# Copies of U and the scaled key moved from VectorE to ScalarE in the mixing of a hybrid encoder

## The chip, the cores and the metric

The kernel runs on one core of a Trainium2 chip. The metric is the device time of one execution in microseconds (us), lower is better. A core has five engines that run side by side, each in the order of its own queue, and that wait for each other through semaphores: TensorE (PE in the profile, PEld its weight loads) multiplies matrices into PSUM; VectorE (DVE) and ScalarE (ACT) work elementwise and carry results out of PSUM; GpSimd (POOL) and SyncE (SP) issue transfers here.

## The reference

Two residual layers on 256 tokens of width 2048. The first mixes with an RWKV-7 recurrence over 32 heads of 64, the second with sparse attention; each is followed by a SwiGLU. The change is in the recurrence alone. Cut to that:

```python
def _rwkv7_scan(r, w, k, v, kk, a):
    def step(S, inp):
        r_t, w_t, k_t, v_t, kk_t, a_t = inp
        sa = jnp.einsum('bhij,bhj->bhi', S, -kk_t)
        S = (S * w_t[:, :, None, :]
             + sa[..., None] * (kk_t * a_t)[:, :, None, :]
             + v_t[..., None] * k_t[:, :, None, :])
        y = jnp.einsum('bhij,bhj->bhi', S, r_t)
        return S, y
...
    kk = heads(k * k_k)
    kk = kk / jnp.maximum(jnp.linalg.norm(kk, axis=-1, keepdims=True), 1e-12)
    k = k.astype(f32) * (1 + (a - 1) * k_a)
    y = _rwkv7_scan(r_h, w_h, k_h, v_h, kk, a_h)
```

The line `k * (1 + (a - 1) * k_a)` is the key that is scaled. Everything is float32.

## The kernel before

The program is a chain of phases. Before and after the mixing stand large linear layers, whose weights SyncE streams in, ScalarE and VectorE split into a high and a low part, and TensorE multiplies. The mixing (`rwkv`) computes the recurrence in chunks of 64 tokens: within a chunk through triangular matrices, between chunks through a state S.

It runs in eight rounds, i = 0 to 7. A round holds two column tiles, j = 0 and 1, of 128 columns (two heads each), and its 256 tokens as NC = 4 chunks. All rounds are written out, so that each engine has one straight list of instructions. A round has three stages on each engine, `stage_M`, `stage_N`, `stage_C`:

- `stage_M`: TensorE multiplies the decayed keys with each other, VectorE masks the result (XE, Dd, W).
- `stage_N`: the triangular inverse grows in W by repeated products. TensorE makes the powers DX2, DX4, D8B, TZ16, TZ32 and the turned values VK in PSUM; ScalarE copies them out (`evac`); VectorE adds to W (`grow`). In the same stage the next round's inputs are prepared (`prep_...` with i + 1): ScalarE makes q (`prep_v`) and the copies vb (`prep_values`) and the exponentials (`prep_exp`); VectorE runs `prep_a` (a running sum Ls) and `prep_b`, which makes the scaled key in the tile k2 (named `k` in the profile): first `a * k_a + (1 - k_a)`, line 2181, with the two columns `pv` and `omka`, then that times k, line 2164, then rb, line 2185.
- `stage_C`: the chain over the four chunks c. TensorE makes R, ScalarE copies it into Rr; TensorE multiplies it into U, VectorE copies it into Uu (line 2308); TensorE makes S and part of the output from Uu, ScalarE copies S scaled (line 2126); then the next chunk. In chunk 0 ScalarE also takes the next round's key norm (`prep_norm`: two logarithms, two exponentials, tile rk). In between VectorE prepares the next round (`prep_d`, `prep_e`) and does the modulation sums (`ada_half`, line 1954, tile `ada_ring`), eight in a round, whose rows SyncE loads. At the end of the stage ScalarE rounds an earlier round's y (`rounded`, tile hid) and then takes y out of PSUM (`take_y`, tile yc).

Nothing but these lists sets the order: an engine whose next instruction waits for a semaphore holds back all behind it. The helpers `at` and `past` write such waits; each instruction adds to a semaphore of its own name ("U", "S", "t1" for the scaled key).

Of the kernel before, what the change touches and what calls it, by code (L numbers as in the profile page):

```python
# [18 lines left out]
HD = 64  # L19
# [1548 lines left out]
class Program:  # L1568
# [22 lines left out]
    def s(self, name):  # L1591

        if name not in self.sems:
            self.sems[name] = self.nc.alloc_semaphore(name)
        return self.sems[name]
# [300 lines left out]
    def rwkv(self, loras):  # L1896
# [116 lines left out]
        def scalar(act):  # L2013
            def copy(name, dst, src, scale=1.0):
                nc.scalar.activation(dst, src, ACT.Copy, scale=scale).then_inc(s(name), 1)  # L2015
# [14 lines left out]
            def prep_values(i):  # L2030
                for j in range(2):
                    past(act, i, "VK")
                    copy("vb", R[j]["vb"][:], R[j]["in"][:, 2, :])

            def prep_exp(i):
                for j in range(2):
# [79 lines left out]
            def stage_C(i, post, prep):  # L2116
                for c in range(NC):
                    for j in range(2):
                        act.wait_ge(s("Rp"), i * 8 + (2 * c + j + 1))
                        copy("R", R[j]["Rr"][:], bank(j, 2, slice(c * HD, (c + 1) * HD)))  # L2120
                    if prep and c == 0:
                        prep_norm(i + 1)
                    if c < NC - 1:
                        for j in range(2):
                            act.wait_ge(s("Sp"), i * 6 + (2 * c + j + 1))
                            nc.scalar.activation(R[j]["S"][:], bank(j, 1, slice(c * HD, (c + 1) * HD)), ACT.Copy,
                                                 scale=R[j]["Pi_end"][:, c:c + 1]).then_inc(s("S"), 1)
                    elif post:
                        rounded(i - 1)
# [32 lines left out]
        def vector(dve):  # L2162
# [3 lines left out]
            def col(i, first, j):  # L2166
                return self.pv[:, bass.ds(i * 2 + (first + j), 1)]
# [7 lines left out]

            def prep_b(i, j):
                b = R[j]
                r, k, v, sw, a = (b["in"][:, n, :] for n in range(5))
                at(dve, i, "Ls", j)
                tt("Lx", b["Px"][:], b["Ls"][:], sw, SUB)  # L2180
                nc.vector.tensor_scalar(b["k2"][:], a, col(i, PV_KA, j), self.omka[:, bass.ds(i * 2 + j, 1)], MUL, ADD).then_inc(s("t1"), 1)
                at(dve, i, "t1", j)
                tt("k2", b["k2"][:], b["k2"][:], k, MUL)
                at(dve, i, "k2", j)
                nc.vector.scalar_tensor_tensor(b["rb"][:], r, col(i, PV_RK, j), b["k2"][:], MUL, MUL).then_inc(s("rb"), 1)
# [117 lines left out]

            def stage_C(i, q, post, prep):
                for c in range(NC):
                    for j in range(2):
                        dve.wait_ge(s("Up"), i * 8 + (2 * c + j + 1))
                        nc.vector.tensor_copy(R[j]["Uu"][:], bank(j, 3, slice(c * HD, (c + 1) * HD))).then_inc(s("U"), 1)
                    if c == 0:
                        if prep:  # L2310
                            for j in range(2):
                                prep_d(i + 1, 1 - q, j)
                        ada_sums(i)
                    if c in (1, 2) and prep:
                        prep_e(i + 1, 1 - q, c - 1)
                    if prep and c % 2:
                        adas(i + 1, c // 2)
                    if c == 2 and post:
                        gated(i - 1)
# [341 lines left out]
```

## Time and profile before

| | |
|---|---|
| median of the runs | 2681.77 us (2675.21 to 2682.4) |
| the profiled execution, first to last instruction (span) | 2683.1 us |
| mean granted TensorE clock | 0.987 |
| TensorE busy | 2569.3 us, 96% |
| VectorE busy | 1912.7 us, 71% |
| ScalarE busy | 1234.6 us, 46% |

The mixing's rounds lie between 387 and 723 us of the span. How the rows below are read: a *window* gives one stretch (us from the span's start) with its length, the busy time of PE, PEld, DVE, ACT and POOL (number of instructions in brackets), the granted TensorE clock as a share of full speed, the share of the DMA engines and GB/s. A row of *waits* gives who stood idle at which line, for whom, how long in total, how often, and the longest. A row of a *tile* gives an instruction with its count, its shortest, median and longest duration in ns and when the first and the last began. A row of a *timeline* gives start and duration in us, engine, line, operation, what is written from what, how many instructions are merged, and in square brackets the idle time of the engine just before and who ended it; without brackets the engine did not idle. "issue" is idle time for which the profile shows no one to wait for. Durations overlap a little from one instruction to the next.

### The profile page before, as it was taken

The numbers are of one execution on the slowest core, as the hardware profiler recorded it, in microseconds if no ns is written. First come the engines' busy times: TensorE is split into PE (matmuls) and PEld (weight loads), VectorE is DVE, ScalarE is ACT, GpSimd is POOL, SyncE is SP. The second block draws the span as 40 slices with busy tenths as digits, with TensorE's granted clock in tenths as the row PEclk, the third lists the DMA queues.
The fourth block names the chain that finished last, engine by engine and source line by source line (L and its number), as shares of the span: only waits on it lengthen the run. The fifth ranks groups of instructions, "written<-read, shape, count | busy, mean of one in ns | idle before, by whom it ended". The sixth has DMA issues, their size and how long they took to land.

```text
span 2683.1 us, 53108 instructions
## 1 busy us (share of the span) xinstructions
PE 2569.3 (96%) x20028; PEld 2254.2 (84%) x20028; DVE 1912.7 (71%) x2641; ACT 1234.6 (46%) x1886; POOL 46.5 (2%) x83
## 2 busy tenths in 40 slices
PE   7999998888899999999999999999999999999998
PEld 6888887778788888888888888887888888888887
DVE  6868746878687777777777776587887655555556
ACT  2245554444445444444444454344454444444445
POOL 2000020000000000000000000000000000000000
PEclk9999999999999999999999999999999999999999
DMA  9999775444196888888888668656788655666654
GB/s 402 414 327 308 258 255 175 149 152 133 55 318 218 283 284 290 278 282 282 294 278 283 218 220 282 235 207 208 261 282 281 211 189 182 188 195 189 186 164 141
DMA packets 443443, 640.96 MB, mean 239 GB/s; under 512 B 22049, under 2 KB 403105, under 8 KB 422433
## 3 DMA queue, kind: packets, MB, share of 16 engines
q1 hardware_dynamic: 439552, 626.35, 69.3%
q0 software_dynamic: 3744, 12.59, 1.3%
q8 instruction: 101, 1.65, 0.3%
q14 instruction: 46, 0.37, 0.0%
HBM read 624.18 MB, written 14.68 MB: 238 GB/s over the span
## 4 chain that ended last, share of the span: by engine, by line
PE 66%; DVE 4%; ACT 1%; DMA 1%; issue 1%; DVEq 0%; SPq 0%; ACTq 0%
PE ps L1784 43%; PE ps L1788 21%; DVE ada_ring L1830 1%; DVE wlo L1768 1%; DMA ada_ring<-in_ada 1%; ACT whi L1763 1%; DVE nt L131 0%; PE ps L1424 0%; PE ps L1418 0%; DVE act L144 0%; DVE st L1325 0%; PE ps L1457 0%; DVE lgf L1322 0%; PE ps L1449 0%; PE ps L1439 0%
## 5 line engine op out<-in xcount | busy, mean ns | idle before, releaser
L1768 DVE TENSOR_TENSOR wlo<-raw,whi 128x1024 fp32r<-128x1024 f32 (+1 forms) x736 | 865.8, 1192 | 444.6 <-ACT whi L1763 443.1
L1784 PE MATMUL ps<-act,whi 128*128 128x512 f32 x3528 | 1108.4, 395 | 1.6 <-DVE act L144 1.6
L1763 ACT ACTIVATE whi<-raw 128x1024 fp32r<-128x1024 f32 (+1 forms) x736 | 745.5, 1030 | 643.7 <-PE ps L1788 637.7
L1788 PEld LDWEIGHTS ps<-act,wlo 128*128 128x128 f32 x3528 | 662.7, 188 | 156.6
L1788 PE MATMUL ps<-act,wlo 128*128 128x256 f32 x3528 | 693.2, 278 | 0.0
L1784 PE MATMUL ps<-hid,whi 128*128 128x512 f32 x2176 | 680.7, 394 | 8.3 <-DVE wlo L1768 7.3
L1784 PEld LDWEIGHTS ps<-act,whi 128*128 128x128 f32 x3528 | 537.3, 189 | 2.4 <-DVE wlo L1768 2.0
L1788 PEld LDWEIGHTS ps<-hid,wlo 128*128 128x128 f32 x2176 | 410.3, 189 | 89.7
L1788 PE MATMUL ps<-hid,wlo 128*128 128x256 f32 x2176 | 433.0, 279 | 0.0
L1784 PEld LDWEIGHTS ps<-hid,whi 128*128 128x128 f32 x2176 | 332.3, 189 | 10.9 <-DVE wlo L1768 4.9
L1830 DVE SCALAR_TENSOR_TENSOR ada_ring<-ada_ring,silu 128x2048 f32<-128x2048 f32 x128 | 292.4, 2285 | 12.3 <-DMA ada_ring<-in_ada 12.3
L1133 PE MATMUL ps<-first_mix,raw 128*128 (+1 forms) x512 | 114.5, 386 | 7.0 <-DVE first_mix L1007 7.0
L1133 PEld LDWEIGHTS ps<-first_mix,raw 128*128 128x128 f32 x512 | 98.4, 193 | 23.1 <-issue 5.0
L93 ACT ACTIVATE small<-ps 128x512 f32<-128x512 f32 x164 | 95.2, 580 | 28.2 <-PE ps L1788 28.2
L390 ACT ACTIVATE hid<-hf 128x512 f32 (+1 forms) x44 | 27.8, 632 | 138.4 <-DVE hf L404 138.4
L1954 DVE SCALAR_TENSOR_TENSOR ada_ring<-ada_ring,silu 128x1024 f32<-128x1024 f32 x64 | 77.2, 1216 | 2.5 <-DMA ada_ring<-in_ada 2.5
L2015 ACT ACTIVATE DX<-ps 128x512 f32<-128x512 f32 x64 | 37.8, 593 | 64.6 <-PE ps L2364 64.4
L387 ACT ACTIVATE sig<-sgt 128x512 f32<-128x512 f32 x44 | 27.8, 632 | 80.3 <-DVE sgt L98 80.3
L407 DVE TENSOR_TENSOR hid<-hf,hid 128x512 f32 (+1 forms) x44 | 30.5, 693 | 44.6 <-ACT hid L390 44.6
L331 DVE SCALAR_TENSOR_TENSOR x<-gsum,mod,x 128x256 f32 (+1 forms) x120 | 52.9, 482 | 12.1 <-DVE gsum L98 11.5
L314 ACT ACTIVATE tmp<-x 128x512 f32 (+1 forms) x28 | 17.7, 632 | 92.9 <-DVE x L331 92.9
L2164 DVE TENSOR_TENSOR W<-W,ps 128x256 f32<-128x256 f32 x80 | 32.9, 420 | 29.4 <-PE ps L2364 28.2
(269 smaller groups left out, 2180.8 us busy)
## 6 DMA issues: line engine op xcount, KB each, us to landing
raw<-in_f_w SPq DMA_DIRECT2D x480, 512.0 KB, 4.6
ada_ring<-in_ada SPq DMA_DIRECT2D x144, 1024.0 KB, 7.6
raw<-in_a_w_rkv SPq DMA_DIRECT2D x96, 512.0 KB, 7.7
ada_ring<-in_ada SPq DMA_DIRECT2D x64, 512.0 KB, 4.1
raw<-in_b_w_in SPq DMA_DIRECT2D x56, 512.0 KB, 3.9
raw<-in_f_w SPq DMA_DIRECT2D x64, 384.0 KB, 4.0
first_ring<-in_ada SPq DMA_DIRECT2D x16, 1024.0 KB, 12.7
raw<-in_a_w_o SPq DMA_DIRECT2D x32, 512.0 KB, 7.8
```

What stands on the lines that cost most here:

```text
L93: p.nc.scalar.activation(self.small[:, g], p.ps[:, 2 * g:2 * g + 2, T:2 * T], ACT.Copy).then_inc(p.s(f"small_out{g}"), 1)
L331: last = p.nc.vector.scalar_tensor_tensor(p.x[:, bass.ds(m, 1), :], p.gsum[:, g, b:b + 1, :], p.mod[:, bass.ds(m + 16 * self.gate, 1)], p. ...
L407: nc.vector.tensor_tensor(p.hid_lo[:, bass.ds(i * 2, 2), :], p.hf[:], p.hid_hi[:, bass.ds(i * 2, 2), :].bitcast(F32), SUB).then_inc(s("hid ...
L1133: last = nc.tensor.matmul(p.ps[:, 4 * h + m // 2, (m % 2) * T:(m % 2 + 1) * T], p.raw[:, u, m * P:(m + 1) * P], src[:, bass.ds(k, 1), :].r ...
L1763: self.nc.scalar.activation(self.whi[:, u % SPL, 0:n], self.raw[:, u, 0:n], ACT.Copy).then_inc(self.s("hi_ready"), 1)
L1768: self.nc.vector.tensor_tensor(self.wlo[:, u % SPL, 0:n], self.raw[:, u, 0:n], self.whi[:, u % SPL, 0:n].bitcast(F32), SUB).then_inc(self. ...
L1784: self.nc.tensor.matmul(self.ps[0:c1 - c0, banks[b], :], hi[:, kk, c0:c1], src[:, k].rearrange("p a t -> p (a t)"), start=k == 0, stop=False)
L1788: last = self.nc.tensor.matmul(self.ps[0:c1 - c0, banks[b], T:2 * T], lo[:, kk, c0:c1], src[:, k, 0, :], start=False, stop=k == ktotal - 1)
L1830: self.nc.vector.scalar_tensor_tensor(tile, tile, 1.0, self.silu[:], MUL, MUL, accum_out=self.mod[:, bass.ds(r * 2 + (a + j), 1)]).then_in ...
L1954: nc.vector.scalar_tensor_tensor(place(n), place(n), 1.0, self.silu[:, (n % 2) * W:(n % 2 + 1) * W], MUL, MUL, accum_out=self.parts[:, n:n ...
L2015: nc.scalar.activation(dst, src, ACT.Copy, scale=scale).then_inc(s(name), 1)
L2164: nc.vector.tensor_tensor(out, a, b, op).then_inc(s(name), 1)
```

## The change

Two pieces of work move from VectorE's list to ScalarE's. The scaled key's first step (a times a column plus a column) leaves `prep_b` and joins `prep_values`, behind the copies vb of both tiles; VectorE's product with k now waits for it. The copies of U, two per chunk, leave VectorE's `stage_C` and stand in ScalarE's, behind R and, in chunk 0, behind `prep_norm`, and before S. TensorE's list is the same.

```diff
             def prep_values(i):
                 for j in range(2):
                     past(act, i, "VK")
                     copy("vb", R[j]["vb"][:], R[j]["in"][:, 2, :])
+                for j in range(2):
+                    past(act, i, "ka")
+                    nc.scalar.activation(R[j]["k2"][:], R[j]["in"][:, 4, :], ACT.Identity, scale=col(i, PV_KA, j),
+                                         bias=self.omka[:, bass.ds(i * 2 + j, 1)]).then_inc(s("t1"), 1)
...
                     if prep and c == 0:
                         prep_norm(i + 1)
+                    for j in range(2):
+                        act.wait_ge(s("Up"), i * 8 + (2 * c + j + 1))
+                        copy("U", R[j]["Uu"][:], bank(j, 3, slice(c * HD, (c + 1) * HD)))
                     if c < NC - 1:
...
             def prep_b(i, j):
                 b = R[j]
-                r, k, v, sw, a = (b["in"][:, n, :] for n in range(5))
+                r, k, v, sw = (b["in"][:, n, :] for n in range(4))
                 at(dve, i, "Ls", j)
                 tt("Lx", b["Px"][:], b["Ls"][:], sw, SUB)
-                nc.vector.tensor_scalar(b["k2"][:], a, col(i, PV_KA, j), self.omka[:, bass.ds(i * 2 + j, 1)], MUL, ADD).then_inc(s("t1"), 1)
                 at(dve, i, "t1", j)
...
             def stage_C(i, q, post, prep):
                 for c in range(NC):
-                    for j in range(2):
-                        dve.wait_ge(s("Up"), i * 8 + (2 * c + j + 1))
-                        nc.vector.tensor_copy(R[j]["Uu"][:], bank(j, 3, slice(c * HD, (c + 1) * HD))).then_inc(s("U"), 1)
```

ScalarE in chunk 0 of a round's `stage_C` (Rr, Uu and S are the chain's copies of R, U and S, rk the norm of the next round's key; the digit behind a name is the tile j). Before:

```order
L2015 ACTIVATE Rr0_140<-ps 128x64
L2015 ACTIVATE Rr1_174<-ps 128x64
L2048 ACTIVATE rk0_132<-rk0_132 128x256
L2048 ACTIVATE rk1_166<-rk1_166 128x256
L2051 ACTIVATE rk0_132<-rk0_132,cst_74 128x256
L2051 ACTIVATE rk1_166<-rk1_166,cst_74 128x256
L2126 ACTIVATE S0_142<-ps,Pi_end0_143 128x64
L2126 ACTIVATE S1_176<-ps,Pi_end1_177 128x64
```

The same place on ScalarE after the change:

```order
L2015 ACTIVATE Rr0_140<-ps 128x64
L2015 ACTIVATE Rr1_174<-ps 128x64
L2052 ACTIVATE rk0_132<-rk0_132 128x256
L2052 ACTIVATE rk1_166<-rk1_166 128x256
L2055 ACTIVATE rk0_132<-rk0_132,cst_74 128x256
L2055 ACTIVATE rk1_166<-rk1_166,cst_74 128x256
L2015 ACTIVATE Uu0_141<-ps 128x64
L2015 ACTIVATE Uu1_175<-ps 128x64
L2133 ACTIVATE S0_142<-ps,Pi_end0_143 128x64
L2133 ACTIVATE S1_176<-ps,Pi_end1_177 128x64
```

The two copies of U have come in between the norm's last exponential and S; on VectorE they stood in front of `prep_d`, with no norm ahead of them.

ScalarE in the middle of `stage_N` (VK, DX and yr come out of PSUM, vb is a copy of the next round's v, k the scaled key). Before:

```order
L2015 ACTIVATE VK0_120<-ps 128x512
L2015 ACTIVATE VK1_154<-ps 128x512
L2015 ACTIVATE vb0_125<-in0_107 128x256
L2015 ACTIVATE vb1_159<-in1_108 128x256
L2015 ACTIVATE DX40_118<-ps 128x512
L2015 ACTIVATE DX41_152<-ps 128x512
```

The same place on ScalarE after the change:

```order
L2015 ACTIVATE VK0_120<-ps 128x512
L2015 ACTIVATE VK1_154<-ps 128x512
L2015 ACTIVATE vb0_125<-in0_107 128x256
L2015 ACTIVATE vb1_159<-in1_108 128x256
L2036 ACTIVATE k20_134<-in0_107,omka_72,pv_70 128x256
L2036 ACTIVATE k21_168<-in1_108,omka_72,pv_70 128x256
L2015 ACTIVATE DX40_118<-ps 128x512
L2015 ACTIVATE DX41_152<-ps 128x512
```

The scaled key of both tiles stands between v and DX4, behind the two evacuations of VK.

VectorE in the same stage, around the key (Px from the running sum, rb the key times r, W the growing inverse). Before:

```order
L2164 TENSOR_TENSOR Px0_130<-Ls0_127,in0_107 128x256
L2181 TENSOR_SCALAR k20_134<-in0_107,pv_70,omka_72 128x256
L2164 TENSOR_TENSOR k20_134<-k20_134,in0_107 128x256
L2185 SCALAR_TENSOR_TENSOR rb0_135<-in0_107,pv_70,k20_134 128x256
L2164 TENSOR_TENSOR Px1_164<-Ls1_161,in1_108 128x256
L2181 TENSOR_SCALAR k21_168<-in1_108,pv_70,omka_72 128x256
L2164 TENSOR_TENSOR k21_168<-k21_168,in1_108 128x256
L2185 SCALAR_TENSOR_TENSOR rb1_169<-in1_108,pv_70,k21_168 128x256
L1954 SCALAR_TENSOR_TENSOR ada_ring_55,parts_75<-ada_ring_55,silu_57 128x1024
L2164 TENSOR_TENSOR W0_122<-W0_122,ps 128x256
L2164 TENSOR_TENSOR W1_156<-W1_156,ps 128x256
```

The same place on VectorE after the change:

```order
L2171 TENSOR_TENSOR Px0_130<-Ls0_127,in0_107 128x256
L2171 TENSOR_TENSOR k20_134<-k20_134,in0_107 128x256
L2191 SCALAR_TENSOR_TENSOR rb0_135<-in0_107,pv_70,k20_134 128x256
L2171 TENSOR_TENSOR Px1_164<-Ls1_161,in1_108 128x256
L2171 TENSOR_TENSOR k21_168<-k21_168,in1_108 128x256
L2191 SCALAR_TENSOR_TENSOR rb1_169<-in1_108,pv_70,k21_168 128x256
L1954 SCALAR_TENSOR_TENSOR ada_ring_55,parts_75<-ada_ring_55,silu_57 128x1024
L2171 TENSOR_TENSOR W0_122<-W0_122,ps 128x256
L2171 TENSOR_TENSOR W1_156<-W1_156,ps 128x256
```

The two scalings are gone, and the first step on k is now the product, which waits for ScalarE; the modulation sum and W stand behind it as before.

## Rows read from the trace of the kernel before

**Rows 1.** Windows of two stretches of the mixing, each as long as a round.

```profile
460.00:500.10 40.10, 33.49 (x882) 30.68 (x879) 32.60 (x80) 19.85 (x54) 0.00 (x0) 1.00 0.45 146
500.10:540.20 40.10, 35.27 (x901) 32.61 (x898) 32.59 (x81) 19.69 (x54) 0.00 (x0) 0.96 0.46 147
```

**Rows 2.** Waits in the mixing, 380 to 730 us, four of the list.

```profile
PE ps L2364 <- issue: 41.8, 26, 3.0
DVE Uu L2308 <- PE ps L2364: 33.4, 40, 3.4
PE ps L2364 <- DVE W L2164: 4.6, 10, 1.0
PE ps L2364 <- DVE Uu L2308: 2.4, 7, 0.5
```

**Rows 3.** Tiles Rr and in: R's copy, the scaled key, q.

```profile
L2015 ACT ACTIVATE Rr<-ps x64: 224/224/225, 421.0 to 718.5; 128x64 f32<-128x64 f32 x64
...
L2181 DVE TENSOR_SCALAR k<-in,pv,omka x14: 404/408/411, 397.9 to 654.3; 128x256 f32<-128x256 f32 x14
L2025 ACT ACTIVATE q<-in,pv x14: 492/493/509, 389.1 to 645.6; 128x256 f32<-128x256 f32 x14
```

**Rows 4.** Timelines, chunk 0 of rounds 2 and 7: VectorE, ScalarE, TensorE.

```profile
503.62 0.23 DVE L2308 COPY Uu<-ps 128x64 f32<-128x64 f32 x1
...
504.92 0.50 ACT L2126 ACTIVATE S<-ps,Pi_end 128x64 f32<-128x64 f32 x2
...
505.36 0.33 PE L2364 MATMUL ps<-S,rho_al 64*64 64x64 f32 x4 [0.22 <-ACT S L2126]
...
709.95 0.23 DVE L2308 COPY Uu<-ps 128x64 f32<-128x64 f32 x1
...
710.77 0.32 ACT L2126 ACTIVATE S<-ps,Pi_end 128x64 f32<-128x64 f32 x1 [0.83 <-PE ps L2364]
```

**Rows 5.** Timelines, chunk 2 of round 2: VectorE, TensorE.

```profile
509.57 0.35 DVE L2308 COPY Uu<-ps 128x64 f32<-128x64 f32 x2
...
509.93 0.33 PE L2364 MATMUL ps<-Uu,D8B 64*64 64x64 f32 x4 [0.49 <-DVE Uu L2308]
```

**Rows 6.** Timelines, stage N of round 1: VectorE, ScalarE, TensorE.

```profile
444.63 0.41 DVE L2181 TENSOR_SCALAR k<-in,pv,omka 128x256 f32<-128x256 f32 x1
445.08 0.42 DVE L2164 TENSOR_TENSOR k<-k,in 128x256 f32<-128x256 f32 x1
...
447.58 1.22 DVE L1954 SCALAR_TENSOR_TENSOR ada_ring<-ada_ring,silu 128x1024 f32<-128x1024 f32 x1
...
446.82 1.21 ACT L2015 ACTIVATE DX<-ps 128x512 f32<-128x512 f32 x2
...
449.36 0.63 PE L2364 MATMUL ps<-DX 64*64 64x64 f32 x16
...
452.59 1.15 PE L2364 MATMUL ps<-W,D8B 64*64 64x64 f32 x32 [0.27 <-DVE W L2164]
```

**Rows 7.** Timelines, stage N of round 3: VectorE, TensorE.

```profile
529.62 1.22 DVE L1954 SCALAR_TENSOR_TENSOR ada_ring<-ada_ring,silu 128x1024 f32<-128x1024 f32 x1
...
533.25 1.15 PE L2364 MATMUL ps<-W,D8B 64*64 64x64 f32 x32 [0.78 <-DVE W L2164]
```

**Rows 8.** Timelines, end of the last round: ScalarE, VectorE, TensorE.

```profile
718.66 0.71 ACT L2077 ACTIVATE hid<-yo 128x256 fp32r<-128x256 f32 x2
...
721.28 0.23 DVE L2308 COPY Uu<-ps 128x64 f32<-128x64 f32 x1 [2.16 <-PE ps L2364]
...
722.76 2.07 PE L2396 MATMUL ps<-yr,blk 128*128 128x256 f32 x4 [0.78 <-ACT yr L2062]
```

**Rows 9.** Timeline of TensorE, end of round 2 and stage M of round 3.

```profile
513.48 0.27 PE L2364 MATMUL ps<-VK,BF 64*64 64x64 f32 x1 [2.55 <-issue]
...
515.99 1.94 PE L2364 MATMUL ps<-rho_al,be 64*64 64x128 f32 x16
...
518.27 1.05 PE L2364 MATMUL ps<-rho_al,be 64*64 64x128 f32 x16
```

## The prediction

> **What bounds the kernel now.** I read the page's first two parts, then windows of single rounds of the mixing, then the list of waits, then the timelines of the three engines around the edited lines. Outside the mixing nothing is edited, so everything is decided in its eight rounds (one for each pair of 128-wide column tiles), 40.1 us apart and lying between 387 and 723 us.
>
> In a round TensorE is busy for 33.5 to 35.3 us, VectorE for 32.6, ScalarE for less than 20 [rows 1]. VectorE and TensorE look alike there, so the shares don't say who bounds; the waits do [rows 2]. VectorE waits for TensorE before 40 of its 64 copies of U alone, 33.4 us in all. TensorE waits for VectorE's W 10 times, 4.6 us in all, and for its U 7 times, 2.4 us. Its largest idle item is "issue", 41.8 us, gaps in which it waits for nothing the profile shows. So the rounds are a chain through TensorE; VectorE and ScalarE matter only where TensorE stands waiting for one of them. Relieving VectorE is worth what it takes out of the 4.6 and the 2.4 us, 7.0 us at the very most, and loading ScalarE costs wherever a copy in the chain then stands behind other work.
>
> **The change part by part.** Durations first [rows 3]. ScalarE's copy of R, the same shape and source as U, takes 224 ns; VectorE's copy of U takes 0.23 us [rows 4]. The copy itself costs nothing to move. VectorE's scaled key takes 408 ns, and no row shows it on ScalarE. The nearest row is the q activation of the same size with one column operand, 493 ns; the new one has two (scale and bias). I bound it by 493 ns from below and 0.6 us from above, and take 0.58, since from R to S, one column more at 64 wide, it goes from 0.224 [rows 3] to 0.32 [rows 4]. The second of a pair ends about 0.5 later, so ScalarE gets 1.07 us more in a round.
> The Trainium skill, ScalarE: Activation LUTs, What ACT_TABLE_LOAD costs, gives 186 ns + 0.833 ns per element and about 93 ns for each column operand, an estimate of 585 ns here; with 493 ns in its place the key's term below would be 0.5 us smaller. The same page, Rules for kernel authors, says to put mul and add on VectorE: that speaks against this half of the change.
>
> *Copies of U, chunk 0.* On ScalarE they now stand behind the two logarithms and two exponentials of the next round's norm (the order shows it, in the section on the change). Before, in round 2, VectorE copied U at 503.62, well inside that block; S was the first to come out of it, at 504.92, with no idle time in front of it, and TensorE stood 0.22 us for S [rows 4]. Now U comes out of the block at 504.92 and S follows by the step U, product, S. In the last round, which has no norm, that step is 709.95 to 710.77, 0.82 us [rows 4]. So S comes 0.82 us later, and TensorE with it. The pattern (S straight behind the norm) stands in five of the seven rounds with a norm; in one of them an issue gap covers 0.2. In the other two an issue gap holds TensorE beyond the norm anyway: nothing. Sum 5 x 0.82 - 0.2 = **+3.9 us**. It can't be less than 0 here, nor more than 7 x 0.82 = 5.7.
>
> *Copies of U, later chunks.* VectorE had them behind a 1.22 us sum of the modulation: in chunk 2 of round 2 U comes at 509.57 with no idle time in front of it, and TensorE stands 0.49 us for it [rows 5]. ScalarE is idle there. Two rounds have this (0.49 and 0.50) and one stands 0.41 in its last chunk: **-1.4 us**; the floor of the gain is 0, the ceiling the 2.4 of [rows 2]. Other waits for U are answered in one copy's time on either engine.
>
> *The scaled key.* VectorE made it itself, at once. Now its product k waits for ScalarE, where the pair stands behind both evacuations of VK and both copies of v, in the place where the evacuation of DX4 began. In round 1 that is at 446.82; 0.58 and 0.05 of hand-over later, at 447.45, VectorE can multiply, where it did at 445.08 [rows 6]. It gets there at 444.63, where the scaling stood, and so waits 2.8 us with the rest of its queue behind it: the key's second product, rb, the next sums and the additions to W for which TensorE waits. From there to its next modulation sum took 2.50 us (to 447.58); without the scaling (one step of 0.45, from 444.63 to 445.08) 2.05. So the sum starts at 449.50 instead of 447.58.
> Whether that reaches TensorE is read from round 3, where VectorE is late already: sum at 529.62, and TensorE gets W for its fourth product at 533.25 after a wait of 0.78 [rows 7], 3.63 later. So in round 1 TensorE would get it at 453.13, not 452.59 [rows 6]: +0.54. Rounds 1, 2, 5 and 6 are alike (ScalarE 0.6 to 1.9 us late on the sum). In rounds 3 and 4 VectorE was later than ScalarE now is: there the saved step brings the sum forward and gives 0.36 and 0.22 back. Round 0 ends in an issue gap either way. Together 4 x 0.54 - 0.6 = **+1.6 us**; at 493 ns +1.1, at 0.6 us +1.7.
> The evacuation of DX4, 1.21 us from 446.82, ends 1.07 later, at 449.1; TensorE takes it at 449.36 [rows 6]. The cover is 0.26 us; were it gone, each round would cost what is over.
>
> *The end.* In the last round the rounding of y (0.71 us the pair, at 718.66) moves behind U, of which the second copy starts only at 721.28; ScalarE then takes y late, and TensorE stands 0.78 us for the square already [rows 8]. **+0.4 us**, between 0 and 0.7.
>
> *What hides.* VectorE no longer waits for U and runs through the end of each round ahead; the next thing it does waits for TensorE's masks, so nothing is gained. SyncE's loads of the modulation rows and tiles, issued when VectorE is done with the old ones, go out a few us earlier; VectorE's sums show no idle time in front of them as it is [rows 6, 7], so that is worth nothing. Ahead of round 0 the key is made once in the same way; VectorE then idles for TensorE's sums anyway, and uncovered it would cost the 1.07 us once.
>
> Sum: 3.9 - 1.4 + 1.6 + 0.4 = **+4.5 us** on a profiled span of 2683.1. The median of the runs is 2681.77, 1.3 below that span, so 2686.3.
>
> **The rivals.**
> *TensorE falls to its low clock more often (slower).* Of the two stretches of [rows 1] one shows a granted clock of 1.00, the other 0.96: a stretch of it ran at 1.2 instead of 2.4 GHz, behind an issue gap of 2.55 us, and 16 matmuls of one kind took 1.94 us there and 1.05 after it [rows 9]. It costs at most 0.04 x 40.1 = 1.6 us a round. The new 0.8 us of standing in chunk 0 comes in the same part of a round as those gaps. For it: TensorE stands longer before. Against: in chunk 0 it already stood 0.22 and more without falling. It decides from three more such stretches: 2686.3 + 3 x 1.6 = 2691; with five, 2694.
> *The issue gaps swallow the new waits.* If TensorE's code is loaded ahead while it stands, a wait before a gap shortens the gap, and the +3.9 and +1.6 vanish: 2681.8 - 1.4 + 0.4 = 2681. For it: there are two or three gaps in every round, 41.8 us. Against: the gap of 2.55 us [rows 9] comes in the chunk after the wait of 0.49 [rows 5], and it is not short: the longest of the 26 has 3.0 [rows 2].
> The Trainium skill, Runtime: NRT & Kernel Launch, Instruction fetch mechanics, says that code comes in blocks fetched while the last one runs and that crossing a block is mostly hidden; no view of mine ties the gaps to it, and 41.8 us are not hidden.
> *VectorE is the bound (faster).* It gives up 8 copies of 0.23 and two scalings of 0.41 in a round, 2.6 us, some 20 us in all: 2662. Against it stand the 33.4 us for which it waits before U alone.
>
> **How the numbers follow.** A measurement of this kernel tells about 0.3% from no change, 8 us. My forecast, a small loss of 1 to 8 us, gets 0.70; the low clock 0.14 (2688 to 2697); the gaps 0.13 (2678 to 2683); VectorE as the bound 0.03. Slower by over 8 us (above 2689.8) is most of the second and the upper edge of the first: 0.14. Faster by over 8 us is the last and a little of the third: 0.04. Within, 0.82. The likeliest time is 2686.3; the bounds of the terms are 0 - 2.4 + 1.1 + 0 = -1.3 at one end (2680.5) and 5.7 - 0 + 1.7 + 0.7 = 8.1 at the other (2689.9), and with about half of the second and of the third case the range is 2678 to 2692.5.
>
> **What would show it.** Right: in chunk 0 ScalarE's U starts straight behind the norm and S 0.8 us later than now relative to U's product; VectorE's k waits for ScalarE by 2 us in four rounds; TensorE's waits for VectorE's U and ScalarE's late chunks disappear, its waits for U of chunk 0 appear; rounds of about 40.6 us; VectorE's busy time falls by about 20 us with no gain. Wrong: rounds shorter than 39.5 us, evacuations of DX4 for which TensorE stands, or granted clocks of a round under 0.9.

## The result and the profile after

| | before | after |
|---|---|---|
| median of four runs | 2680.45 us | 2692.61 us (2690.17 to 2696.31) |
| difference of the medians | | +12.2 us |
| ratio, 95% interval | | 1.0047 (1.0035 to 1.0060), +9.4 to +16 us |
| span of the profiled execution | 2683.1 us | 2691.2 us |
| VectorE busy | 1912.7 us | 1893.3 us |
| ScalarE busy | 1234.6 us | 1253.0 us |

The median of before is that of four runs; the 2681.77 us from which the forecast starts was that of the first three. A second set of four runs of after gave the same: 1.0043 (1.0027 to 1.0058), +11.5 us. So the change costs about 12 us, where 4.5 were forecast: the sign was right, the size was not, and 2692.61 lies just above the range.

All of it is in the mixing: TensorE's first product there starts at 386.5 us in both profiles, and from its first product behind the mixing to the end it takes 1958.5 us before and 1959.2 after. The windows below go from the same TensorE instruction to the same TensorE instruction, from the start of round 0's chain to the last product of the chains, before and then after (columns as in [rows 1]):

```profile
421.45:721.98 300.53, 255.18 (x6485) 236.83 (x6484) 226.75 (x557) 141.61 (x383) 0.00 (x0) 0.95 0.40 129
```

```profile
420.26:729.58 309.32, 258.51 (x6484) 240.86 (x6484) 208.47 (x480) 157.54 (x458) 0.00 (x0) 0.93 0.38 125
```

It grew by 8.8 us: TensorE's busy time by 3.3 at a granted clock of 0.93 instead of 0.95, the rest is idle time. A profile is one execution, and executions differ: the second profiles, of which more below, have 296.1 us for this window before and 314.7 after. The waits of after, 380 to 740 us (to be set beside [rows 2]), and behind them one of before that is not there, 380 to 730 us:

```profile
DVE XE L2171 <- PE ps L2367: 67.2, 16, 10.4
PE ps L2367 <- issue: 41.8, 23, 4.0
ACT Uu L2015 <- PE ps L2367: 16.8, 33, 4.5
PE ps L2367 <- ACT Uu L2015: 7.0, 11, 1.0
PE ps L2367 <- DVE W L2171: 6.1, 9, 1.0
DVE k L2171 <- ACT k L2036: 3.8, 7, 1.1
```

```profile
DVE XE L2164 <- PE ps L2364: 16.2, 16, 3.6
```

TensorE now stands 7.0 us for U on ScalarE, where it stood 2.4 for U on VectorE, and 6.1 instead of 4.6 for W. "issue" is 41.8 us again, but in fewer and longer gaps: up to 4.0 us instead of 3.0. That the sums are equal is chance: in the second profiles "issue" is 36.3 us before and 47.2 after, and W is 5.5 and 6.1. And VectorE waits 67.2 us, up to 10.4 at a time, in front of XE, the first thing that it does in a round's stage M, instead of 16.2: it has run far ahead. By the means of two profiles each the window grew by 13.7 us: TensorE's busy time by 3.5, its waits for U by 5.1 and for W by 1.1, "issue" by 5.5.

Where in a round the time went is seen by cutting the seven rounds that have a successor into three stretches: chunk 0 (from its first Rr to that of chunk 1), from there to VectorE's first XE, and from XE to the next round's first Rr (stages M and N). Sums over the seven rounds, from the starts of these instructions in the timelines, of two profiles of either kernel and of the experiments told of below:

```
                                     chunk 0   to XE   XE to Rr
before                                 27.5     80.8     179.4
before, second profile                 24.3     82.9     178.0
after                                  31.6     88.3     178.5
after, second profile                  30.0     91.1     179.8
U alone (e1)                           31.8     87.7     175.6
key alone (e2)                         26.9     81.9     178.4
U of chunks 1 to 3 alone (e3)          27.0     84.7     175.2
U of chunk 0 alone (e14)               29.4     82.0     181.4
after, norm behind S (e4)              34.6     82.9     176.2
after, VectorE paced (e5)              30.6     83.9     176.0
U of chunks 1 to 3, paced (e7)         28.6     84.5     176.9
after, loads held (e11)                29.7     83.0     178.8
U of chunks 1 to 3, loads held (e13)   27.0     81.2     180.3
before, loads held (e12)               26.7     82.7     182.7
after, short tiles (e6)                29.3     84.2     176.4
before, short tiles (e8)               24.9     76.3     175.8
after, loads cut (e9)                  29.7     75.3     171.9
before, loads cut (e10)                23.1     81.4     172.7
```

Chunk 0 costs 4.9 us by the means of two profiles each (25.9 to 30.8); the stretch from chunk 1 to XE 7.9 us (81.9 to 89.7); stages M and N, where the key is, nothing that can be told (178.7 to 179.2). The prediction had the first, and had a gain in the second. The experiments have one profile each, and two profiles of one kernel differ by 2.4 to 2.5 us in the sum of a row and by up to 3.2 in one column, so a row is a hint; what an experiment costs is told by its runs.

Chunk 0 after the change, ScalarE and then TensorE in round 2, as [rows 4]:

```profile
510.20 0.90 ACT L2055 ACTIVATE rk<-rk,cst 128x256 f32<-128x256 f32 x2
511.00 0.32 ACT L2015 ACTIVATE Uu<-ps 128x64 f32<-128x64 f32 x2
511.72 0.31 ACT L2133 ACTIVATE S<-ps,Pi_end 128x64 f32<-128x64 f32 x1 [0.40 <-PE ps L2367]
```

```profile
511.35 0.33 PE L2367 MATMUL ps<-Uu,D8B 64*64 64x64 f32 x4 [0.98 <-ACT Uu L2015]
```

U starts straight behind the norm, with no idle time, and S 0.72 us behind U. TensorE stands 0.98 us for U, and it does so in six rounds.

Now the stretch to XE. In round 1 TensorE's last product before a gap, the product behind it, SyncE's issues and the window ahead of the gap with the DMA share, after:

```profile
475.43 0.31 PE L2367 MATMUL ps<-rho_al,S 64*64 64x64 f32 x4
479.79 0.48 PE L2367 MATMUL ps<-Rr,W 64*64 64x64 f32 x4 [4.04 <-issue]
...
468.88 0.38 SPq L1970 DMA_DIRECT2D in<-scr  x1
...
471.49 0.37 SPq L1970 DMA_DIRECT2D in<-scr  x1
...
472.89 0.91 SPq L1986 DMA_DIRECT2D g<-scr  x2
474.06 0.92 SPq L1965 DMA_DIRECT2D ada_ring<-in_ada  x2
...
470.35:475.75 5.40, 4.33 (x123) 3.98 (x123) 3.47 (x10) 2.58 (x10) 0.00 (x0) 1.00 0.90 276
```

The same place before:

```profile
471.70 0.31 PE L2364 MATMUL ps<-rho_al,S 64*64 64x64 f32 x4
474.41 0.33 PE L2364 MATMUL ps<-Rr,W 64*64 64x64 f32 x4 [2.40 <-issue]
...
467.49 0.38 SPq L1970 DMA_DIRECT2D in<-scr  x1
...
471.43 0.37 SPq L1970 DMA_DIRECT2D in<-scr  x1
...
473.70 0.90 SPq L1986 DMA_DIRECT2D g<-scr  x2
474.87 0.33 SPq L1965 DMA_DIRECT2D ada_ring<-in_ada  x1
...
466.60:472.00 5.40, 4.32 (x123) 3.98 (x123) 4.44 (x13) 2.11 (x8) 0.00 (x0) 1.00 0.38 121
```

Both kernels stop at the same instruction, where a 16 KB piece of code comes in on the queue that the page calls "q8 instruction". What differs is what the DMA engines do just then. Before, the two tiles of the next round go out 3.9 us apart and gates and modulation rows follow at 473.70: in the 5.4 us ahead of the gap the DMA share is 0.38. After, the tiles follow each other within 2.6 us and gates and rows come right behind: in the 5.4 us ahead of the gap the share is 0.90. In the trace's record of that queue the packet for this place starts at 477.23, 1.49 us after TensorE has run dry; before it started 0.07 us after.

There is one such place in each of rounds 0 to 6. The seven gaps add up to 13.0 and 13.7 us in the two profiles of before and to 21.5 and 23.7 in those of after. Over these seven places in each of the 18 profiles (before, after and experiments), 126 in all, TensorE went on 2.2 to 3.1 us behind the start of the code packet in nineteen of twenty. Where the DMA engines had been busy for less than 30% of the 1.4 us ahead of that packet, the gap was 1.75 us on average (63 places, the longest 2.74); where they had been busy for more than 70%, 2.91 us (55 places, the longest 4.17). The eight places in between do not all fit: the two longest gaps of all, 4.74 and 4.72 us, stand behind DMA engines that were a third busy. Nor is a short burst enough: in the second profile of before round 1's packet has a share of 0.93 in the 1.4 us ahead of it, with 0.37 over the 5.4 us ahead of the gap, and the gap is 2.12 us.

### The profile page after: what moved, and what is told of

Its sections match the earlier page's. It is cut to its first block, busy times and chain, and to the rows that moved or that the text cites. A ratio compares the mean times of both kernels' runs of the same rounds, so it can differ in the third digit from the quotient of the medians.

```text
span 2691.2 us, 53108 instructions
## 1 busy us (share of the span) xinstructions
PE 2571.8 (96%) x20028; PEld 2256.6 (84%) x20028; DVE 1893.3 (70%) x2561; ACT 1253.0 (47%) x1966; POOL 46.2 (2%) x83
## 4 chain that ended last, share of the span: by engine, by line
PE 66%; DVE 4%; ACT 1%; DMA 1%; issue 1%; DVEq 0%; SPq 0%; ACTq 0%
PE ps L1784 43%; PE ps L1788 21%; DVE ada_ring L1830 1%; DVE wlo L1768 1%; DMA ada_ring<-in_ada 1%; ACT whi L1763 1%; DVE nt L131 0%; PE ps L1424 0%; PE ps L1418 0%; DVE act L144 0%; DVE st L1325 0%; PE ps L1457 0%; DVE lgf L1322 0%; PE ps L1449 0%; PE ps L1439 0%
## 5 line engine op out<-in xcount | busy, mean ns | idle before, releaser
L1830 DVE SCALAR_TENSOR_TENSOR ada_ring<-ada_ring,silu 128x2048 f32<-128x2048 f32 x128 | 292.5, 2285 | 11.6 <-DMA ada_ring<-in_ada 11.5
L331 DVE SCALAR_TENSOR_TENSOR x<-gsum,mod,x 128x256 f32 (+1 forms) x120 | 52.9, 482 | 12.1 <-DVE gsum L98 11.5
L2171 DVE TENSOR_TENSOR XE<-ps,m_XE 128x512 f32<-128x512 f32 x16 | 11.1, 692 | 67.2 <-PE ps L2367 67.2
```

Of the source, the lines that this page charges most:

```text
L331: last = p.nc.vector.scalar_tensor_tensor(p.x[:, bass.ds(m, 1), :], p.gsum[:, g, b:b + 1, :], p.mod[:, bass.ds(m + 16 * self.gate, 1)], p. ...
L1830: self.nc.vector.scalar_tensor_tensor(tile, tile, 1.0, self.silu[:], MUL, MUL, accum_out=self.mod[:, bass.ds(r * 2 + (a + j), 1)]).then_in ...
```

## The experiments

Three theories stood at first: W, the time follows TensorE's named waits and the rest is chance; C, chunk 0's standing brings the low clock; K, the key is behind most of it. After the first four runs none of them could explain the loss, and F took their place: **VectorE, freed of U, runs ahead, the loads that it releases go out in a bunch at the end of the chain, and TensorE's code, a transfer too, comes late.** Against it stood L (low clock or chance) and later G (the gaps come late by the pace of the copies, loads or not). Times below are ratios to the kernel before on the same chip, turned into us, with 95% intervals; its median there was 2681.4 to 2684.8.

**e1: the copies of U alone.** `prep_b` and `prep_values` as before:

```diff
-                for j in range(2):
-                    past(act, i, "ka")
-                    nc.scalar.activation(R[j]["k2"][:], ...)
...
+                nc.vector.tensor_scalar(b["k2"][:], a, col(i, PV_KA, j), ...)
```

> Only the copies of U move to ScalarE; the scaled key stays on VectorE. Against the kernel before. Theory W (the time follows TensorE's named waits, and the low clock is chance): chunk 0 +5.2 us, later chunks -1.3, end +0.2, so +4.1 us, and the clock may come out either way. Theory C (the longer standing in chunk 0 moves TensorE's issue gaps and with them brings the low clock): the same waits and some 3 us on top, +7 us, with a granted clock 0.002 below the kernel before. Theory K (the key, which holds VectorE's queue, is behind most of the loss): +2 us or less. By W and C the profile shows TensorE waiting 0.98 us for ScalarE's U of chunk 0 in six rounds, and its waits for VectorE's W as before (4.1 us).

+8.0 us (4.3 to 11.8). The gaps in rounds 0 and 1 are 3.37 and 3.77 us, as in after, and U of chunk 0 is waited for 0.98 us. But TensorE's wait for W in stage N is 0.78 us here too, with the key on VectorE (round 1's stage N; e1, then after):

```profile
499.30 0.92 PE L2364 MATMUL ps<-W,D8B 64*64 64x64 f32 x24 [0.78 <-DVE W L2167]
```

```profile
499.26 0.45 PE L2367 MATMUL ps<-W,D8B 64*64 64x64 f32 x8 [0.78 <-DVE W L2171]
```

The waits for W are 5.8 us in all here, 6.1 with the key alone (e2) and in after, and 5.5 in the second profile of before: the 0.78 is not the key's doing, and the rise in the sum is hardly more than what two profiles differ by. U is most of the loss.

**e2: the key alone** (the other half of the diff).

> Only the scaled key moves to ScalarE; the copies of U stay on VectorE. Against the kernel before. Theory W: +1.8 us, TensorE's waits for VectorE's W 5.9 us instead of 4.1. Theory C: +1.8 us and the clock of the kernel before. Theory K: most of the 9 us that the mixing grew, +6 us or more.

+1.1 us (-1.3 to +3.8). K falls.

**e3: the copies of U of chunks 1 to 3 alone.**

```diff
+                    if c > 0:
                         for j in range(2):
                             act.wait_ge(s("Up"), i * 8 + (2 * c + j + 1))
                             copy("U", ...)
```

> Only the copies of U of chunks 1 to 3 move to ScalarE; that of chunk 0 and the key stay on VectorE. Against the kernel before. Theories W and C: -1.3 us for the later chunks and +0.2 at the end, so -1.1 us, no wait of 0.98 us in chunk 0, and the clock as before. Theory K: the same. If the low clock comes with any shift of the copies, the time rises by some 3 us although the waits fall.

+6.4 us (2.4 to 10.2), where all theories had -1 (with some 3 us of low clock as a reservation). TensorE's waits for U are down to 0.7 us in all, as they should be, and still it is slower. That is the finding that made F: something behind the copies, not the copies. The profile of this run does not show the loss, though: its seven gaps are longer (18.3 us), but its window over the chains is 299.9 us, against 300.5 and 296.1 before, and its row in the table adds up to 286.9 us, against 287.7 and 285.2.

**e4: the norm behind S.**

```diff
-                    if prep and c == 0:
-                        prep_norm(i + 1)
...
                     elif post:
                         rounded(i - 1)
+                    if prep and c == 0:
+                        prep_norm(i + 1)
```

> The whole change, with the next round's key norm (two logarithms, two exponentials) placed behind the copies of S in chunk 0 instead of ahead of U. Against the kernel before. Theory W: the 5.2 us of chunk 0 go, and the 0.22 us for which TensorE stood for S in three rounds go too: -0.7 - 1.3 + 1.8 + 0.2 = 0 us. Theory C: 0 us, and the clock comes back to that of the kernel before. Theory K: +4 us or more, since the key is still on ScalarE. The norm comes 1.2 us later to VectorE, which waited for it once; nothing is expected from that.

+9.9 us (6.7 to 13.4): no help. The norm, 1.6 us long, has no room behind S either; TensorE's wait moved to chunk 1's R. Its waits, 380 to 732 us:

```profile
PE ps L2367 <- ACT Rr L2015: 6.3, 7, 0.9
PE ps L2367 <- ACT Uu L2015: 0.8, 4, 0.3
```

**e5 and e7: VectorE held to the old pace**, in e5 with the whole change, in e7 with e3's copies:

```diff
                 for c in range(NC):
+                    dve.wait_ge(s("Up"), i * 8 + (2 * c + 2))
```

> The whole change, and VectorE's list waits for TensorE's U product at the place where its copies of U stood, without copying. It so prepares the next round at the old pace, and SyncE's loads of tiles, gates and modulation rows go out at the old times. Against the kernel before. Theory F (VectorE, freed of U, runs ahead, the loads that it releases go out in one bunch, and TensorE's next block of code, fetched by a transfer too, waits behind them; the gaps of TensorE that were covered by VectorE's work in the next stage now come ahead of it, uncovered): only the waits of chunk 0 and the key remain, +3 to +6 us, and the gaps of rounds 0 and 1 ahead of XE are back at 1.5 and 2.4 us from 3.6 and 4.0. Theory L (the loss beyond the waits is low clock by standing in chunk 0, or chance): +8 to +12 us as with the change, and gaps of 3 us and more.

> The copies of U of chunks 1 to 3 on ScalarE, chunk 0 and the key on VectorE, and VectorE's list waits in chunks 1 to 3 for U's product as before, without copying. Against the kernel before. Theory F: the 5.6 us that the same kernel without these waits lost are gone and the 1.3 us of the late chunks remain as a gain: -1 us. Theory L: +5 us, since neither the clock nor the copies are touched by the waits.

e7: +2.9 us (0.0 to 5.9), about half of e3's loss, where F had -1. e5: +9.7 us (6.2 to 12.9), outside what F had said and inside what L had. In e5 VectorE no longer runs ahead (it waits 20.0 us in front of XE, as before), and the time is lost all the same: this speaks against that part of F. In both the first gap is short again (1.18 and 0.87 us, with idle DMA engines ahead of the code's packet), but others stay at about 3 and more (in e5 2.97, 3.01 and 3.56, behind DMA engines 87% busy and more): at the old pace the loads still meet the code in some rounds.

**e6 and e8: short tiles**, in the changed kernel and in the kernel before. From round 2 on the tiles are loaded for one of 128 partitions, so these two leave most of their input out:

```diff
-                    projected(i, j)
-                    low_rank(i, j)
+                    for q0, q1 in ((0, 3), (3, 5)):
+                        sp.dma_start(R[j]["in"][0:1, q0:q1], ...)
```

> The whole change, but from round 2 on the tiles of the next round are loaded for one partition of 128 only, so that the mixing computes with old inputs in the others; every instruction and every wait is there. It takes away most of the transfers that go out while VectorE runs ahead. To be set against the kernel before with the same short loads. Theory F: it differs from that by the waits alone, +3 to +6 us, and its gaps ahead of XE in rounds 0 to 4 are 2.5 us or less. Theory L: +8 us or more, with gaps of 3 us and more left.

> The kernel before, with the same short loads of the tiles from round 2 on. Theory F: the loads cost TensorE little at their old times, so 0 to -3 us against the kernel before, and its gaps stay at 1 to 2 us. Theory L: 0 us.

e6: +6.2 us (2.9 to 9.4); e8: -7.2 us (-9.9 to -4.3). They stay 13 us apart, and e8 gains more than the 3 us that F allowed: F's numbers missed. In e6's trace gates and modulation rows still go out in a bunch, and the gaps of 2.55 and 4.04 us in rounds 0 and 1 lie behind DMA engines some 85% busy. The seven gaps add up to 17.9 us in e6 and 11.8 in e8, which is 6 of the 13 us; chunk 0 is 4.4 longer. So the short tiles had taken away only a part of the loads that count, and more of it in the kernel before.

**e9 and e10: all loads of the mixing cut** to one partition, gates and modulation rows too, behind the first ones.

> The whole change, and all loads of the mixing after its first ones (tiles from round 2 on, gates from round 1 on, modulation rows from round 1 on) fetch one partition of 128; VectorE's modulation sum has the factor 0.125 for 1.0, so that old rows don't grow. What is computed is therefore not the reference; every instruction and wait is there. To be set against the kernel before, cut in the same way. Theory F (the loss beyond chunk 0 is TensorE's code fetched late, behind loads that go out in one bunch since VectorE runs ahead): without loads only chunk 0 and the key are left, +4 to +6 us, and the stretches from chunk 1 to XE are as long in both, within 1 us in all. Theory G (the gaps come late by the pace of the copies themselves, loads or not): +11 us or more, with the stretches to XE 6 us longer in all, as between the two kernels with short tiles (13 us).

> The kernel before, with the same cut of all the mixing's loads. Theory F: faster than the kernel before by 7 us as with short tiles, or by some us more, up to 12. Theory G: no more than with short tiles, -7 us.

e9: -9.4 us (-12.9 to -5.9), median 2673.1; e10: -15.3 us (-18.8 to -11.5), median 2666.2. Without loads the change costs 5.9 us by these two ratios (6.9 between the medians); with them, on the same chip, 11.5. In the chains e9 has no gap of 2.8 us, and the seven gaps add up to 12.9 us in e9 and 12.6 in e10: the same. TensorE's "issue" of the whole mixing, 380 to 725 us, e9 and then e10:

```profile
PE ps L2375 <- issue: 29.4, 20, 3.1
```

```profile
PE ps L2372 <- issue: 28.3, 18, 2.5
```

With loads it was 41.8 and 47.2 us in after, 41.8 and 36.3 in before. So the longer gaps need the loads, and G falls; what is left of the change is a little more than chunk 0 and the key were given. F's other number missed: the stretches to XE were to be equal within 1 us, and e9's are 6.1 us shorter than e10's, its chunks 0 6.6 longer. Both windows over the chains are 289 us long; the profile of e10 is its slowest run (2672.3, the other four 2665.0 to 2666.7), so the two profiles do not show where the difference of the medians lies.

**The second profiles** of both kernels as they are.

> The kernel before once more, for a second profile: how far TensorE's gaps and the low clock differ between two executions of one kernel. Theory F: ahead of XE gaps of 1 to 2.6 us as in the first, none of 3 us or more in rounds 0 and 1, and the stretches from chunk 1 to XE within 2 us of the first in all. Theory L (chance): gaps of 3 us and more appear here too.

> The kernel with the change once more, for a second profile and for times on the same chip as its cut forms. Theory F: +10 to +13 us against the kernel before, with gaps of 3 us and more ahead of XE in rounds 0 and 1 again and the stretches from chunk 1 to XE 6 us longer in all. Theory L (chance): the gaps sit elsewhere, and their sum before XE is that of the kernel before.

c1 has no gap over 2.8 us in a chain (first fence, round 1's place); c2 has one of 4.74 in round 0 (second fence), and 3.24, 3.02, 3.38 and 4.17 in later rounds. So the long gaps are the change's and not chance: that half of L falls.

```profile
473.29 0.33 PE L2364 MATMUL ps<-Rr,W 64*64 64x64 f32 x4 [2.12 <-issue]
```

```profile
439.20 0.48 PE L2367 MATMUL ps<-XE,Uu 64*64 64x64 f32 x4 [4.74 <-issue]
439.47 1.92 PE L2367 MATMUL ps<-rho_al,be 64*64 64x128 f32 x16
```

The second row of c2 shows where the clock comes in: behind the long gap 16 products take 1.92 us that take 1.05 at full clock [rows 9].

**e11, e12, e13: the bunch held back.** Gates and two modulation rows wait for the next round's XE; VectorE stays free. e11 is the whole change, e12 the kernel before, e13 e3's copies:

```diff
             def gates(i):
-                    past(sp, i, "yg")
+                    at(sp, i + 1, "XE", 0)
...
             ada(i + 1, 4, 5)
-                        sp.wait_ge(s("ada_half"), i * HALVES + (n - 3))
+                        at(sp, i, "XE", 0)
```

> The whole change, with SyncE holding the loads of the gates and of two modulation rows (4 and 5) until VectorE has written the next round's XE, so that they no longer go out in a bunch with the tiles at the end of the chain; VectorE runs ahead as with the change. Against the kernel before. Theory F: the bunch is shorter by 1.2 MB of loads, so the gaps of TensorE ahead of XE are below 2.6 us and the loss falls from 12 to +5 to +8 us. Theory G (the gaps are late by the pace of the copies, loads or not): +10 to +13 us, gaps of 3 us and more as with the change.

> The kernel before, with the same loads held. Against the kernel before. Theory F: at the old pace these loads go out at the end of the chain too, partly behind the last fetch of code, so 0 to -4 us. Theory G: 0 us.

> The copies of U of chunks 1 to 3 on ScalarE, chunk 0 and the key on VectorE, with the same loads held. Against the kernel before. Theory F: the +5.6 us of these copies without the hold are gone, 0 to -4 us. Theory G: +5 us as without the hold.

e11: +2.7 us (-1.3 to +6.7) where the change had cost 11.5 to 12.2; F had said +5 to +8. e13: 0.0 us (-3.5 to +3.2) where e3 had cost 6.4. e12: -1.3 us (-4.6 to +1.9). This is the clearest of the tests: two waits of SyncE, and nothing on ScalarE or VectorE, take most of the loss away, and they do not speed up the kernel before. (Each is compared with the kernel before on its own chip; e3 and the second set of the change without the hold ran on others.) The windows of e11 and, behind it, of the changed kernel's second profile, between the same two instructions as above:

```profile
421.14:724.50 303.36, 254.16 (x6484) 235.86 (x6484) 208.45 (x480) 157.67 (x458) 0.00 (x0) 0.96 0.40 128
```

```profile
422.09:736.75 314.66, 259.13 (x6485) 241.30 (x6484) 208.10 (x480) 157.19 (x458) 0.00 (x0) 0.93 0.38 123
```

Not all fits: of e11's seven gaps four are still over 3 us (tiles meet the code there), 19.3 us in all, where after has 21.5 and 23.7 and before 13.0 and 13.7, so the gaps alone do not explain what came back. Against the mean of after's two profiles the window is 8.6 us shorter: TensorE's busy time, at a clock of 0.96, is 4.7 us lower, the seven gaps 3.3. For e3 and e13 the windows tell no difference (299.9 and 300.1 us). None of the versions that load everything beats the kernel before by what can be measured.

**e14: chunk 0's copies alone.**

```diff
+                    if c == 0:
                         for j in range(2):
                             act.wait_ge(s("Up"), i * 8 + (2 * c + j + 1))
                             copy("U", ...)
```

> Only chunk 0's copies of U move to ScalarE, behind the norm; those of chunks 1 to 3 and the key stay on VectorE, which is so kept at the old pace. Against the kernel before. Theory F: chunk 0 alone, +4 to +6 us, TensorE waiting 0.98 us for U in six rounds, gaps as before. Theory G: +7 us or more, with gaps of 3 us and more in rounds 0 and 1.

+2.7 us (-0.3 to +5.4), where F had +4 to +6. Its row of the waits, and its window:

```profile
PE ps L2369 <- ACT Uu L2015: 5.9, 6, 1.0
```

```profile
421.06:726.25 305.19, 255.37 (x6487) 236.43 (x6484) 222.98 (x543) 144.47 (x399) 0.00 (x0) 0.96 0.39 127
```

All six waits of 0.98 us are there, and the clock is 0.96 and the busy time that of before: standing in chunk 0 brought no low clock here. It is not without effect everywhere. In c2, e1, e5, e9 and e11 a stretch at the lower of the two levels, half the full clock, starts within 0.6 us behind one of these waits, with no other gap over 0.5 us in the 4 us ahead; in c2 behind the wait that ends at 595.34 us:

```profile
592.30:595.70 3.40, 2.04 (x50) 1.63 (x46) 2.77 (x11) 2.25 (x9) 0.00 (x0) 1.00 0.49 159
595.70:599.10 3.40, 3.40 (x64) 3.40 (x65) 3.33 (x10) 1.30 (x5) 0.00 (x0) 0.50 0.36 121
```

These are one or two stretches in a profile, and nearly all others stand behind "issue" gaps. So C falls as the cause of the loss and may hold as a small part of it.

## Why the prediction missed

**Bound.** Right: rounds hang on TensorE. VectorE's busy time fell by 19.4 us (20 were said) and nothing was gained by it. But in stages M and N VectorE was nearer to the path than I read: from the second XE to the third W it idles only for k in five of after's seven stretches with a key, and a gap of TensorE in that stretch is covered by it. A gap in front of XE is covered by nothing. In after the gaps behind XE in rounds 0 and 1 (1.45 and 1.87 us before) are gone, and those in front have grown. So behind the equal 41.8 us of "issue" in the first two profiles there is a move from a covered place to an open one, and in the second two "issue" grew besides. That the cover makes the difference is read from the lists and was not tested by itself.

**Chunk 0, +3.9.** Right in mechanism and near in size. U stands behind the norm and S 0.72 us behind U, where 0.82 were said; it happens in six rounds and not in five. Chunk 0 grew by 4.9 us in the profiles; in time it is +2.7 (e14, -0.3 to 5.4).

**Later chunks, -1.4.** Right as a wait (2.4 us for VectorE's U became 1.1 for ScalarE's, 7.0 - 6 x 0.98), wrong as a gain: e3 is 6.4 us slower.

**Key, +1.6.** The new activation takes 586 ns where 580 were said:

```profile
L2036 ACT ACTIVATE k<-in,omka,pv x16: 584/586/596, 375.3 to 660.1; 128x256 f32<-128x256 f32 x16
```

The Trainium skill, ScalarE: Activation LUTs, What ACT_TABLE_LOAD costs, gave an estimate of 585 ns: the measurement agrees.

VectorE's k waits for it 3.8 us in seven waits, of at most 1.1 us and not 2. In round 1 ScalarE reached that place 9.0 us behind the second XE in the profile of before, from which I reckoned; in after it comes 7.2 us behind it, as TensorE's gap in between (1.45 us) is gone there. The alone-run gives +1.1 us (-1.3 to 3.8), the stretch of stages M and N no difference. Near in size, partly by luck: waits for W of 0.78 us in round 1, as I ascribed to it, come without it (e1).

**The end, +0.4.** TensorE stands 1.04 us for the square instead of 0.78: +0.3.

**What hides: the step that failed.** "SyncE's loads of the modulation rows and tiles, issued when VectorE is done with the old ones, go out a few us earlier; VectorE's sums show no idle time in front of them as it is [rows 6, 7], so that is worth nothing." I asked whether the loads would arrive sooner for those who wait for them, and not what else they would meet on the way. They met the packets of TensorE's code, and TensorE's gaps in front of XE grew from 13.0 and 13.7 us to 21.5 and 23.7. With the gates and two of the rows held the loss is 2.7 us (-1.3 to 6.7), near my sum of 4.5 without it; with all loads cut it is 5.9 to 6.9. That loads cost most of what the sum lacks is shown by these runs. That they cost it since VectorE runs ahead is not shown: at the old pace (e5) the loss stayed.

**Rivals.** The low clock did come (0.95 and 0.96 before, 0.93 in both profiles after), by the 3.3 us of busy time that two such stretches cost by my price, and the measured time lies in that rival's range; but for the most part not from standing in chunk 0, as I had it: nearly all low stretches stand behind "issue" gaps, and one in c2 behind the new wait. From the chains' start to the end of the mixing the clock was low for 42 and 41 us in the two profiles of after and for 29 and 26 in those of before. That gaps swallow waits may be right in one place: in round 4 a gap of 1.12 us shrank to 0.11 behind the new wait of 0.98, though the second profile of before has only 0.30 there. It is wrong as a rule. VectorE as the bound is excluded.

The Trainium skill, Runtime: NRT & Kernel Launch, Instruction fetch mechanics, says that crossing a block of code is mostly hidden. This case's traces do not agree in the chains: at all but five of the 126 places TensorE stood idle for 1.1 us and more.

What stays open: why e11 wins back more than its gaps show, and e5 less; why the profiles of e3 and e13 are alike where their times are not; and what makes the clock fall more often. The seven gaps alone do not set it: e7, with 15.1 us of them, has the low clock for 40 us, e11, with 19.3, for 26. That a code packet waits behind loads is inferred from the order of the packets and from e9 to e13; no row names it.

## What to carry to other kernels

When work leaves an engine that is not the bottleneck, list what that engine releases when it runs ahead, loads above all, and look in the windows' DMA share at what those loads will meet. Here it helped to hold the loads (e11), and not to hold the engine (e5). The gaps of TensorE marked "issue" at the same instruction in every run were code coming in here; what they cost depends on what covers them, so compare places and not sums, and take a second profile before reading a sum. A term of the waits table says what a wait costs now, not what the stretch will cost when the wait goes: cut the stretch between the same two instructions in both traces.

## What the runs showed of the hardware

- Cutting the mixing's loads makes the kernel before 15.3 us faster (e10), though its engines show only two waits for a load there, of 3.5 and 2.5 us: TensorE's "issue" fell from 41.8 and 36.3 us to 28.3, so most of the gain is there.
- At the seven places TensorE goes on some 2.4 us (median) after its 16 KB code packet has started, in every kernel here; what varies from -2.3 to +2.4 us is when that packet starts against the moment at which TensorE runs dry.
- Runs of the kernel before spread over 13 us on one chip (2676.5 to 2689.7), with mean clocks of 0.984 to 0.990; two profiles of one kernel differ by 4.4 to 5.3 us in the window over the chains.
- In five profiles a stretch at half the full clock starts within 0.6 us behind a wait of TensorE of 0.98 us; in e14 none does behind six such waits.
